# Scores of two attention mixers as four rounded-format products each, over remainders made by VectorE

## The reference, cut to what matters

```python
# first mixer, 8 heads each, head size 64
s = q @ k.T * 64 ** -0.5; y_a = softmax(where(key <= query, s, -1e30)) @ v
z = q @ k.T * 64 ** -0.5; y_b = stick_breaking(z) @ v
# second mixer
I = sum_h w[h] * relu(q_idx[h] @ k_idx.T)        # 8 index heads, one k_idx
y_a = softmax(q @ k.T * 64 ** -0.5 + cum_t - cum_s) @ v
y_b = softmax(q @ k.T * 64 ** -0.5 + bias, over the 64 best keys of I) @ v
merged = gate_a * (y_a @ w_a) + gate_b * (y_b @ w_b); out = merged @ w_out
```

## Time and profile before

| | |
|---|---|
| median of 3 runs | 1165.41 us (1165.4 to 1166.91) |
| the profiled execution | 1165.56 us, of which the traced span is 1163.7 us |
| PE busy | 1152.2 us, 99% |
| DVE busy | 706.2 us, 61% |
| ACT busy | 546.0 us, 47% |
| M0, M1 in the span | about 204 to 382 us, about 774 to 965 us |

### The profile page before, as it was taken

How to read it: one execution, slowest core, us unless ns; L and a number is a source line. 1 busy time by engine, 2 the same in 40 slices (tenths; PEclk the granted TensorE clock), 3 DMA queues, 4 the chain that set the end, 5 groups by cost and what they waited for, 6 DMA issues and landing times.

```text
span 1163.7 us, 13505 instructions
## 1 busy us (share of the span) xinstructions
PE 1152.2 (99%) x5422; PEld 946.3 (81%) x5422; DVE 706.2 (61%) x911; ACT 546.0 (47%) x626; POOL 51.5 (4%) x94
## 2 busy tenths in 40 slices
PE   7999999999999999999999999999999999999998
PEld 6888888878888888888888888888777888888887
DVE  5555554736787765555485556458798677555542
ACT  4444442655546454444354445346554664444440
POOL 2000000000000000000000000020241100000000
PEclk9999999999999999999999999999999999999999
DMA  9656566553354656555565555657443345655540
GB/s 310 220 184 196 189 222 202 201 169 121 123 185 146 198 183 188 187 197 186 182 198 182 182 193 183 201 157 252 164 145 109 110 153 180 195 187 190 181 181 37
DMA packets 143038, 208.52 MB, mean 179 GB/s; under 512 B 9336, under 2 KB 100616, under 8 KB 142976
## 3 DMA queue, kind: packets, MB, share of 16 engines
q1 hardware_dynamic: 139296, 198.01, 52.0%
q0 software_dynamic: 3248, 9.06, 2.2%
q10 hardware_dynamic: 432, 0.59, 0.2%
HBM read 206.56 MB, written 2.64 MB: 180 GB/s over the span
## 4 chain that ended last, share of the span: by engine, by line
PE 97%; DVE 1%; DMA 1%; ACT 0%; SPq 0%; issue 0%; DVEq 0%; ACTq 0%
PE bank L1394 30%; PE bank L1396 29%; PE bank L1395 29%; PE bank L1503 2%; PE bank L1608 1%; PE bank L1607 1%; DMA raw<-in_ffn_w_up 1%; PE bank L1416 1%; PE bank L1620 1%; PE bank L1579 1%; DVE w_lo L965 1%; PE bank L1648 1%; PE bank L1647 1%; PE bank L1646 0%; PE bank L1604 0%; PE bank L1656 0%
## 5 line engine op out<-in xcount | busy, mean ns | idle before, releaser
L965 DVE TENSOR_TENSOR w_lo<-raw,w_hi 128x2048 fp32r<-128x2048 f32 (+1 forms) x187 | 425.2, 2278 | 222.0 <-ACT w_hi L679 221.4
L1394 PE MATMUL bank<-w_hi,xT_hi 128*128 128x512 f32 (+1 forms) x1112 | 443.1, 398 | 2.9 <-DVE xT_lo L985 2.9
L1396 PE MATMUL bank<-w_hi,xT_lo 128*128 128x512 f32 (+1 forms) x1112 | 432.9, 389 | 0.0
L1395 PE MATMUL bank<-w_lo,xT_hi 128*128 128x512 f32 (+1 forms) x1112 | 432.2, 389 | 0.0
L679 ACT ACTIVATE w_hi<-raw 128x2048 fp32r<-128x2048 f32 (+1 forms) x187 | 354.6, 1900 | 113.2 <-PE bank L1396 109.1
L1394 PEld LDWEIGHTS bank<-w_hi,xT_hi 128*128 128x128 f32 x1112 | 209.2, 188 | 52.5 <-issue 8.6
L1396 PEld LDWEIGHTS bank<-w_hi,xT_lo 128*128 128x128 f32 x1112 | 209.2, 188 | 44.6
L1395 PEld LDWEIGHTS bank<-w_lo,xT_hi 128*128 128x128 f32 x1112 | 209.6, 188 | 40.0
L1394 PE MATMUL bank<-w_hi,hT_hi 128*128 128x512 f32 x352 | 137.7, 391 | 0.0
L1396 PE MATMUL bank<-w_hi,hT_lo 128*128 128x512 f32 x352 | 137.0, 389 | 0.0
L1395 PE MATMUL bank<-w_lo,hT_hi 128*128 128x512 f32 x352 | 137.0, 389 | 0.0
(11 more groups left out here) (247 smaller groups left out, 728.3 us busy)
## 6 DMA issues: line engine op xcount, KB each, us to landing
raw<-in_ffn_w_gate SPq DMA_DIRECT2D x88, 512.0 KB, 4.0
raw<-in_ffn_w_up SPq DMA_DIRECT2D x88, 512.0 KB, 5.0
raw<-in_ffn_w_down SPq DMA_DIRECT2D x88, 512.0 KB, 4.3
raw<-in_w_in SPq DMA_DIRECT2D x76, 512.0 KB, 4.5
raw<-in_w_out SPq DMA_DIRECT2D x16, 512.0 KB, 4.0
raw<-in_w_branch_moba SPq DMA_DIRECT2D x4, 512.0 KB, 4.1
raw<-in_w_branch_sb SPq DMA_DIRECT2D x4, 512.0 KB, 4.2
raw<-in_w_branch_a SPq DMA_DIRECT2D x4, 512.0 KB, 4.3
```

The lines of the kernel that those rows point to most:

```text
L965: dve.tensor_tensor(w_lo[r][:, 0:n], raw[r][:, 0:n], w_hi[u % SLOTS][:, 0:n], ALU.subtract).then_inc(lo_done, 1)
L1394: pe.matmul(dst, st(hi), mhi, start=start, stop=False)
L1395: pe.matmul(dst, st(hi), mlo, start=False, stop=False)
L1396: return pe.matmul(dst, st(lo), mhi, start=False, stop=stop)
```

## The change

Each score becomes four F32R products over all 128 rows. For one operand ("stacked": qa, kb, iq, fq, dq) the 128 rows of a head hold its 64 rounded rows and its 64 remainder rows, in `stat`. The other operand is there twice: its rounded rows in both halves (`twice`), and its remainder in one half with zeros in the other (`rest`). The products `stat` by `twice` and `stat` by `rest` give hi*hi + lo*hi and hi*lo. ACT writes the rounded rows: two copies of 64x512 for a stacked operand, four for another. DVE then takes the remainder from the same bank (`turn_rest`), two operations of 64x512, and only this frees the bank: TR items are now read by "d". A TR item turns four heads (`half`) of all tokens, and the items are ordered anew. POOL zeroes the empty halves of `rest` at the start of each mixer, six fills each.

```diff
@@ -102,15 +102,14 @@
 
 def items_of(b):
     if b == 0:
-        out = [(11, "TR", ("qa", 0)), (11, "TR", ("qa", 1)), (12, "TR", ("ka", 0)), (12, "TR", ("ka", 1))]
+        out = [(11, "TR", ("qa", 0)), (11, "TR", ("ka", 0)), (12, "TR", ("qa", 1)), (12, "TR", ("ka", 1))]
         out += [(t, "SM", ("moba", h)) for h, t in enumerate((14, 15, 17, 18, 19, 21, 22, 23))]
-        out += [(20, "TR", ("qb", 0)), (20, "TR", ("qb", 1)), (24, "TR", ("kb", 0)), (24, "TR", ("kb", 1))]
+        out += [(20, "TR", ("qb", 0)), (20, "TR", ("kb", 0)), (24, "TR", ("qb", 1)), (24, "TR", ("kb", 1))]
         out += [(t, "SB", ("sb", h)) for h, t in enumerate((25, 27, 28, 30, 31, 33, 34, 36))]
     else:
-        out = [(6, "TR", ("iq", 0)), (7, "TR", ("iq", 1)), (11, "TR", ("kk", 0)), (11, "TR", ("kk", 1)),
-               (13, "CU", ())]
+        out = [(6, "TR", ("iq", 0)), (7, "TR", ("iq", 1)), (11, "TR", ("kk", 0)), (13, "CU", ())]
         out += [(12 + h, "IX", h) for h in range(NH)]
-        out += [(15, "TR", ("fq", 0)), (15, "TR", ("fq", 1)), (19, "TR", ("fk", 0)), (19, "TR", ("fk", 1))]
+        out += [(16, "TR", ("fq", 0)), (19, "TR", ("fk", 0)), (20, "TR", ("fq", 1)), (24, "TR", ("fk", 1))]
         out += [(t, "SM", ("fox", h)) for h, t in enumerate((21, 22, 23, 25, 26, 27, 28, 29))]
         out += [(29, "TR", ("dq", 0)), (30, "TR", ("dq", 1))]
         out += [(t, "SM", ("dsa", h)) for h, t in enumerate(range(32, 40))]
+STACKED = ("qa", "kb", "iq", "fq", "dq")
...
-            it.reader = "a" if kind in ("TR", "IX", "CU") else "d"
+            it.reader = "a" if kind in ("IX", "CU") else "d"
...
-        turned_a = ExitStack()
-        with turned_a:
-            yT_a_hi, yT_a_lo = (turned_a.enter_context(nc.sbuf_tensor(n, [P, HW // P, SEQ], F32R))
-                                for n in ("yT_a_hi", "yT_a_lo"))
-        qT_a = mb("qT_a", [P, HW // P, SEQ])
-        kT_a = mb("kT_a", [P, HW // P, SEQ])
-        qT_b = mb("qT_b", [P, HW // P, SEQ])
+        stat = [mb(f"stat{i}", [P, 4, SEQ], F32R) for i in range(2)]
+        twice = [mb(f"twice{i}", [P, 4, SEQ], F32R) for i in range(2)]
+        rest = [mb(f"rest{i}", [P, 4, SEQ], F32R) for i in range(2)]
...
+            def zero_rest():
+
+                for odd, r in ((0, slice(HD, P)), (1, slice(0, HD))):
+                    for half in range(2):
+                        pool.memset(rest[half][r, odd:4:2, :].bitcast(F32), 0.0)
+                    ins = pool.memset(dk_rest[r, odd, :].bitcast(F32), 0.0)
+                ins.then_inc(zeroed, 1)
 
...
+                    if name == "kk":
+                        act.activation(dk_twice[:], S[:, 0:SEQ], ACT.Copy, scale=hg[:, 3:4])
+                        act.activation(ik_twice, S[:, SEQ:2 * SEQ], ACT.Copy).then_inc(qk_hi, 1)
+                        return
+                    scale = scale_of(name)
+                    dst = stat[half] if name in STACKED else twice[half]
+                    for odd in range(2):
+                        r, o = slice(HD * odd, HD * odd + HD), slice(HD * (1 - odd), HD * (1 - odd) + HD)
+                        src = S[r, :].rearrange("p (k t) -> p k t", k=2)
+                        f = scale if isinstance(scale, float) else scale[r]
+                        if name not in STACKED:
+                            act.activation(dst[o, odd:4:2, :], src, ACT.Copy, scale=f)
+                        ins = act.activation(dst[r, odd:4:2, :], src, ACT.Copy, scale=f)
+                    ins.then_inc(qk_hi, 1)
...
+                def turn_rest(it):
+
+                    name, half = it.what
+                    dve.wait_ge(qk_hi, it.trs + 1)
+                    if name not in STACKED:
+                        dve.wait_ge(zeroed, b + 1)
+                    S = bank[4 + it.i % 2]
+                    if name == "kk":
+                        for odd in range(2):
+                            r = slice(HD * odd, HD * odd + HD)
+                            dve.scalar_tensor_tensor(dk_rest[r, odd, :], S[r, 0:SEQ], hg[r, 3:4], dk_twice[r, :],
+                                                     ALU.mult, ALU.subtract)
+                            ins = dve.tensor_tensor(ik_rest[r, odd, :], S[r, SEQ:2 * SEQ], ik_twice[r, :], ALU.subtract)
+                        ins.then_inc(read_d, 1)
+                        return
+                    scale = scale_of(name)
+                    for odd in range(2):
+                        r, o = slice(HD * odd, HD * odd + HD), slice(HD * (1 - odd), HD * (1 - odd) + HD)
+                        src = S[r, :].rearrange("p (k t) -> p k t", k=2)
+                        f = scale if isinstance(scale, float) else scale[r]
+                        hi = (stat if name in STACKED else twice)[half][r, odd:4:2, :]
+                        lo = stat[half][o, odd:4:2, :] if name in STACKED else rest[half][r, odd:4:2, :]
+                        ins = dve.scalar_tensor_tensor(lo, src, f, hi, ALU.mult, ALU.subtract)
+                    ins.then_inc(read_d, 1)
...
+                    c0 += 2 * P * half
+                    for k in range(2):
+                        for tt in range(TT):
+                            ins = pe.transpose(S[:, k * SEQ + tt * P:k * SEQ + (tt + 1) * P],
+                                               xg[:, tt, c0 + k * P:c0 + (k + 1) * P], ident)
                     ins.then_inc(scored, 1)
...
+                    if kind == "idx":
+                        return st, ik_twice, ik_rest[:, h % 2, :]
                     if kind == "dsa":
-                        return qT_b[r, h // 2, :], dkT[r, :], dv[:]
-                    return iqT[r, h // 2, :], ikT[r, :], None
+                        return st, dk_twice[:], dk_rest[:, h % 2, :]
+                    return st, twice[k][:, j, :], rest[k][:, j, :]
+
...
+                    pe.wait_ge(read_d, max(t.read for t in ITEMS[b] if t.kind == "TR" and t.what in halves_of(it)))
                     S = score_bank(it)
-                    q, k, _ = operands(it)
-                    if kind == "sb":
-                        pe.matmul(S[:, 0:SEQ], k[:, 0:P], q, start=True, stop=True)
-                        pe.matmul(S[:, SEQ:SC], k[:, P:SEQ], q[:, P:SEQ], start=True, stop=True).then_inc(scored, 1)
+                    st, m1, m2 = operands(it)
+                    if it.kind == "SB":
+                        pe.matmul(S[:, 0:SEQ], st[:, 0:P], m1, start=True, stop=False)
+                        pe.matmul(S[:, 0:SEQ], st[:, 0:P], m2, start=False, stop=True)
+                        pe.matmul(S[:, SEQ:SC], st[:, P:SEQ], m1[:, P:SEQ], start=True, stop=False)
+                        pe.matmul(S[:, SEQ:SC], st[:, P:SEQ], m2[:, P:SEQ], start=False, stop=True).then_inc(scored, 1)
                     else:
-                        pe.matmul(S[:, 0:P], q[:, 0:P], k[:, 0:P], start=True, stop=True)
-                        pe.matmul(S[:, P:SC], q[:, P:SEQ], k, start=True, stop=True).then_inc(scored, 1)
+                        pe.matmul(S[:, 0:P], st[:, 0:P], m1[:, 0:P], start=True, stop=False)
+                        pe.matmul(S[:, 0:P], st[:, 0:P], m2[:, 0:P], start=False, stop=True)
+                        pe.matmul(S[:, P:SC], st[:, P:SEQ], m1, start=True, stop=False)
+                        pe.matmul(S[:, P:SC], st[:, P:SEQ], m2, start=False, stop=True).then_inc(scored, 1)
```

More of the change, by code:

```diff
@@ L817, in gate_rows, with sum_rows @@
                                        scale=r(tt)).then_inc(gated, 1)
+                def sum_rows(it):
+                    act.wait_ge(scored, it.i + 1)
+                    act.activation(ncum[:], bank[4 + it.i % 2][0:NH, 0:SEQ], ACT.Copy, scale=-1.0).then_inc(read_a, 1)
                 def turn(it):
-                    name, tt = it.what if it.kind == "TR" else ("cu", 0)
+                    name, half = it.what
                     act.wait_ge(scored, it.i + 1)
                     S = bank[4 + it.i % 2]
-                    t = slice(tt * P, (tt + 1) * P)
@@ L905, in mixer @@
                     for it in ITEMS[b]:
[L906 removed]
+                        if slot - it.slot == 1 and it.kind == "TR":
                             turn(it)
+                        if slot - it.slot == 1 and it.kind == "CU":
+                            sum_rows(it)
                         if slot - it.slot == 1 and it.kind == "IX":
@@ L1552, in read_sem, with sum_rows @@
                     return read_d if was.reader == "d" else read_a
+                def sum_rows(it):
+                    pe.wait_ge(rows_ready, 4)
+                    S = score_bank(it)
+                    pe.matmul(S[0:NH, 0:P], lgf[:, 0:8], tri_le, start=True, stop=True)
+                    pe.matmul(S[0:NH, P:SEQ], lgf[:, 0:8], ones, start=True, stop=False)
+                    pe.matmul(S[0:NH, P:SEQ], lgf[:, 8:16], tri_le, start=False, stop=True).then_inc(scored, 1)
                 def turn(it):
-                    name, tt = it.what if it.kind == "TR" else ("cu", 0)
+                    name, half = it.what
```

(9 more changed lines are left out.)

70 lines of the change are left out of this document (30 added, 40 removed).

## The result

The changed kernel takes 1172.98 us (median of four runs, 1172.04 to 1173.47) against 1165.44 us: a ratio of 1.0061, with a 95% interval of 1.0043 to 1.0078. It is 0.6% slower. I had forecast 1164.7 us and a range up to 1169.5.

A forecast was written before the change was run, and what follows sets the result against it. PE, busy 99% of 1163.7 us, was taken as the bound. First mixer -5.8, second to slot 31 +6.2, behind it -4.5, clock +3.4 sum to -0.7 on 1165.56: 1164.9, stated as 1164.7 us against the median; range 1159 to 1169.5.

The forecast's parts named there:

- A score after: 0.46 us: On PE, a score's four products, two of 128 and two of 256 columns, take 0.46 us; bounds 0.36 to 0.52.
- First mixer, -5.8 us, waits of 1.6, 0.5 and 0.5: Lighter scores gain 8.4 us, less 2.6 us of PE waits at slots 12, 21 and 25: net -5.8 us.
- DVE's idle time takes up half of it, so the norm starts at about 821.3.: Second mixer: kk's four remainders cost about 1.6 us, half hidden in idle, so the second row norm moves from 820.44.
- Index head 6 waits 5.8 us: Second mixer: PE, ready at 827.2, waits for fq half 0's remainder, which stands behind the norm and ends at 833.0.
- 4.6 us at slot 31: Second mixer: PE's wait before slot 31's transposes, put at about 4.6 us.
- fk half 0, ready at 842.4: Second mixer: PE turns it at 837.1, ACT's four copies end at 841.0, DVE's remainder at 842.4.
- DVE's waits in this stretch give back 1.7: First softening to last select: 2.8 us of added remainders, 1.7 us recovered from DVE's waits, bringing +5.1 to +6.2 us.
- Behind slot 31, -4.5 us: Second mixer's end: eight DSA scores at 0.56 us each give -4.5 us, with no top-k rounds on DVE.
- The clock, two dips of 1.7: PE's clock halves after the long waits at slots 18 and 31, 1.7 us each; bounds 0 and 3.4.
- (a): Rival: the clock holds, or the waits are shorter than a dip needs, giving 1161.3 us; chance 0.23.
- (b): Rival: DVE hides everything and PE gains 19.5 us over both mixers, giving 1146 us; chance 0.05.
- (c): Rival: GpSimd's zero fills at the mixer seams hold DVE up, 12 x 0.5 = 6 us, giving 1170.7 us; chance 0.17.

The follow-up runs named there:

- m0_only: First mixer as in the changed kernel, second mixer (index, fox and DSA scores, transposes, copies) as in the kernel before: 1159.92 us, ratio 0.996.
- iq1_later: Changed kernel with the remainder of iq, half 1, moved behind the narrow norm chain on DVE: 1169.93 us, ratio 1.0044.
- iq1_fq0_later: iq1_later with fq's half 0 turned in slot 18 instead of 16: 1168.39 us, ratio 1.0027.
- m0_dsa_act: m0_only plus changed DSA heads, dq's halves turned in slots 30 and 31, ACT copying the second ahead of slot 32's split and evacuation: 1154.95 us.
- fill_twice: Changed kernel with GpSimd's zero fills of the second mixer made twice: 1171.83 us, ratio 1.0059.
- one_column: Changed kernel with the second mixer's remainders cut to one column each, score products there reading other operands of the same shape: 1164.49 us, ratio 0.9997.
- the two moves: Changed kernel with iq half 1's remainder behind the narrow norm chain and fk half 0 turned in slot 18 instead of 19: 1163.3 us, ratio 0.9995.
- busy_waits: Changed kernel with products into an unused bank filling PE's waits ahead of index heads 0 (11 products) and 6 (20): 1171.5 us, ratio 1.0056.

## Why the prediction was wrong, step by step

- **A score after: 0.46 us.** Right, in both mixers.
- **First mixer, -5.8 us, waits of 1.6, 0.5 and 0.5.** Right in place and mechanism; the waits were 1.76, 0.84 and 0.87, the stretch -4.9 in the profiled execution and -5.3 by m0_only's median. The longer waits (3.5 us in place of 2.6) are the whole difference. The bounds that I gave for the gain, 7.6 to 10.8 us, do not follow from 0.36 to 0.52 us a score, which makes 7.4 to 10.0; nothing hangs on them.
- **"DVE's idle time takes up half of it, so the norm starts at about 821.3."** This is the step that failed. I costed kk's remainders as work (1.6 us, half of it hidden), put iq's at nothing without a reason, and never asked what stood behind iq's half 1 in DVE's queue while it waited for ACT. It held a split and kk's norm chain, the norm of fk began 4.7 us late (819.56 against 814.9), index head 0 waited 2.94 us where I had none, and a dip followed. iq1_later shows it: same work, the norm at 814.83, 3.05 us back. It is the largest part of the 7.2 us, but not all: with it mended the kernel still takes 1169.93 us, 5.2 us above my forecast. The Trainium skill says it in one clause ("PSUM — Partial Sum Buffer", Engine vs sequencer instructions): the queues of ScalarE and VectorE are strict FIFO. The idle of 3.98 us with runnable work behind it is that rule as a number.
- **Index head 6 waits 5.8 us.** 5.14, close in part by luck, since PE itself came late there; in iq1_later, with the norm where I had put it, the wait is 6.62. (My text has 5.8 in one place and 6.6 in another, and its 4.6 us at slot 31, measured as 4.27, is worked out nowhere.) That it hung on fq's bank alone was too simple, as iq1_fq0_later showed.
- **fk half 0, ready at 842.4.** It was ready at 843.05 with a mixer entered 6.4 us earlier, so 7.0 us late: the 4.7 us above, the dip of 1.7 at half clock, which I had charged apart, and 0.6 us that I can't place. That ACT's four copies there are the handle was half seen; turning fk one slot earlier gave 6.6 us.
- **"DVE's waits in this stretch give back 1.7."** Not so. From first softening to slot 31, 42.5 us became 45.2, 1.6 us more than I had. The remainders did use idle time: they are 3.0 us of work, and DVE's idle time there fell from 2.9 to 1.8 us. What I had not looked for is the split at 860.28 that takes 1.65 us longer beside GpSimd. This term too was mis-sized, at -1.7.
- **Behind slot 31, -4.5 us.** Right in size (m0_dsa_act: 4.2 us from the first mixer on). In the changed kernel it is -2.4 against -2.8, with a dip of 2.5 us in it where I had 1.7.
- **The clock, two dips of 1.7.** The price of one was right for three of them (the last cost 2.5 us), the number was four. I had counted only waits longer than the start's 2.93 us, and of those at 804.58 and 864.96 I had neither.
- **Rivals.** (a) and (b) are out by the trace. (c), the fills, is out by fill_twice (its 1170.7 us, a chance of 0.17, lay outside my own range besides), and by the second mixer's seam, which starts 6.4 us earlier and keeps that offset through all its transposes. The kernel is slower as in (c), by another mechanism that I had no rival for: an operation that waits in a queue in front of others. GpSimd does seem to hold DVE up by 1.65 us, but with the operation at 860.19 and not with a fill.

What stays open: how the 13.1 us of the second mixer divide exactly between order, work and clock. one_column (8.5 us for the work, with waits that shrink along), the two moves (9.7 us) and busy_waits (1.5 to 3.2 us) overlap and do not add up to it. Open too are what decides whether a dip follows a wait, and what the split beside GpSimd costs the whole, which no run takes out.

## What to carry to other kernels

When an operation that waits on another engine is put into an in-order queue, price first what stands behind it and could have run, and only then its own time; here 1.4 us of work cost 3.1 to 3.8 us and 1.4 us of copies 3.7 us by their places alone, clock dips included. A transfer of load from a full engine to engines with "idle time" gives nothing where those engines set the pace in that stretch, so change only those parts whose consumers have slack: the first mixer and the DSA heads, not, in any order tried here, the index and fox heads. And where TensorE is the bound, read the granted clock behind every wait and count both.
